# Six more landing buffers for the weights, in the room of queries, keys and values, until the input units' second halves begin

## The chip, the cores and the metric

The kernel runs on one core of a Trainium2 chip. The metric is the device time of one execution in microseconds (us), given as the median of several runs. TensorE (PE) does the matrix products and the transposes, VectorE (DVE), ScalarE (ACT) and GpSimd (POOL) the rest; SyncE (SP) starts nearly all transfers of weights from device memory (HBM).

## The reference, cut to what matters

Two transformer layers over 256 tokens of width 2048, all in float32. Before the first layer, a vector `c` is turned into six vectors of 2048 that shift, scale and gate its two halves:

```python
mod = silu_c @ w_ada[l] + b_ada[l]                 # w_ada: 2048 x 12288, 100 MB
shift_m, scale_m, gate_m, shift_f, scale_f, gate_f = jnp.split(mod, N_MOD, axis=-1)
h = modulate(rmsnorm(x, g_norm_mix[l]), shift_m, scale_m)
proj = h @ w_in[l]                                 # w_in: 2048 x 3904
...                                                # two kinds of attention, heads of 64 and 128
x = x + gate_m[:, None, :] * mix
h = modulate(rmsnorm(x, g_norm_ffn[l]), shift_f, scale_f)
f = jnp.square(jax.nn.relu(h @ w_ff1[l])) @ w_ff2[l]
```

The second layer projects its input by another `w_in`, runs three attention branches (one of them over the 256 rows of `mem`, by `w_mem_kv`) and projects back.

## The kernel before, in words

All work is written as a Python program that puts instructions into one queue for each engine. An engine works its queue in order; a wait for another engine is a semaphore count.

**Weight tiles.** Every large product is cut into units of up to 512 output columns. A unit runs over pairs of 128 input rows: one pair is a tile of 128 x 1024 numbers (512 KB). Its way: SP starts the transfer into a landing buffer (`fetch`), ACT rounds it to a high part `whi` (line 282), DVE subtracts to get the low part `wlo` (line 283), and PE does twelve products with the high and low parts (lines 392, 393 and 397). `consume` issues transfer and split for a tile four tiles ahead of PE; the split of a tile waits until PE has read the tile four before it. When the split is done, the landing buffer is free. The sixteen tiles of `w_mem_kv` go to PE unsplit.

**Ada parts.** The product with `w_ada` (192 parts of 512 KB in 24 columns `c` of 8) is done on DVE: a part is fetched into a landing buffer like a tile, and one instruction multiplies it by `silu(c)` and sums (line 537, `ada_part`). After the eighth part of a column, small instructions (lines 561 to 566, `ada_reduce`) finish its slice of shift or scale.

**Landing buffers.** They are used in turn: `slot % ring`. While `mem` is projected there are nine, five in `raw` and four in `raw_wide`; `narrow()` then sets the ring to five.

**The order of the work.** `run` lays out a unit tile by tile and calls `pump` after each. `pump` first calls `fill`, which puts ada parts into the queues as long as a model in the program says that the part would be done on DVE at most 3 us after PE: the model keeps a clock for each queue (`PE.t`, `DV.t`, `SP.t`), and one for the transfers (`due["dma"]`), which moves on by 0.00303 us a column, 1.55 us for a full tile or a part, and never starts before SP's clock. A transfer whose landing buffer is free only later holds back SP's clock. Where PE's next pair of inputs (`lhs.ready`) waits for a column of ada, `run` puts the parts that are left of it at once (`wanted`, `ada_token`).

**Around the change.** After the two units of `mem`, `modulated(j)` for j = 0 to 7 makes the inputs of `w_in`, two blocks of 128 rows each: it transposes, scales and shifts by the ada columns (line 781, ACT), and splits (lines 787, ACT, and 789, DVE). Pairs 0 to 3 need ada columns 0, 4, 1, 5; pairs 4 and 5 need 2 and 6; pairs 6 and 7 need 3 and 7. So the first halves of the first six units of `w_in` run first (`u_h0`, 24 tiles on pairs 0 to 3), then two whole units (`u_lat`, eight tiles of 512 and eight of 320 columns on pairs 0 to 7), and then the second halves of the six, mixed with the attention heads. The first unit of `u_lat` thus meets pair 6 after 30 tiles. `region2`, 8192 columns, holds `qT`, `kT`, `dv` (columns 0 to 6143), which are first written after a second half, and `lat` (from column 6144), written after `u_lat`; before it was allotted, its room held the inputs of `mem` and `raw_wide`. `fence` is a list of the last instruction of each queue, on which first writers of reused room wait.

Of the kernel before, what the change touches and what calls it, by code (L numbers as in the profile page):

```python
# [8 lines left out]
F32 = mybir.dt.float32  # L9
# [6 lines left out]
P = 128  # L16
D = 2048
EPS = 1e-6
LAM0 = 0.8 - 0.6 * float(np.exp(-0.0))
NRAW, NSPLIT, NWIDE = 5, 4, 4  # L20
MAGIC = 12582912.0
RSEED = float(0x5F3759DF)
TWO_PI = (6.28125, 1.93500518798828125e-3, 3.0199160510240e-7)
# [111 lines left out]
def program(nc, a, out):  # L135
    with ExitStack() as ctx:
        build(nc, ctx, a, out)


def build(nc, ctx, a, out):  # L140
    def sb(name, shape, dt=F32, scope=ctx):
        return scope.enter_context(nc.sbuf_tensor(name, shape, dt))

    def sem(name):
        return ctx.enter_context(nc.semaphore(name))

    due = {}
    PE, AC, DV, PO = (Queue(sem(f"s_{n}"), due, us) for n, us in (("pe", 0.11), ("act", 0.55), ("dve", 0.3), ("pool", 0.8)))
    SP = Queue(None, due, 0.05)
# [50 lines left out]
    def grab(ring):  # L200

        while all(b.busy for b in ring):
            yield
        b = nxt(ring)
        while b.busy:
            b = nxt(ring)
        b.busy = True
        return b
# [46 lines left out]
    slots = [raw[:, i, :] for i in range(NRAW)]  # L255
    raw_sem = [[sem(f"s_raw{i}"), 0] for i in range(NRAW + NWIDE)]
    raw_free = [[] for _ in raw_sem]
    state = dict(slot=0, ring=NRAW + NWIDE, split=0, nsplit=0, unit=0)
    halves, read = {}, {}

    def fetch(src, n):
# [26 lines left out]
    def narrow():  # L288

        state["ring"], state["slot"] = NRAW, 0  # L290
# [7 lines left out]
    def ada_next():  # L298
        c, k0 = adas.popleft()
        i, x, landed = fetch(a["w_ada"][4 * c + k0 // 4, k0 // 2 % 2], 512)  # L300
        raw_free[i] = [ada_part(x, landed, c, k0)]

    def fill():

        while adas:
            i = state["slot"] % state["ring"]
            if raw_free[i] is None:
                break
            issue = max([SP.t] + [due[id(q), v] for q, v in raw_free[i]])
            landed = max(issue, due.get("dma", 0.0)) + 1.55 + 2.0  # L310
            if max(DV.t, landed) + 1.3 > PE.t + 3.0:
                break
            ada_next()
# [4 lines left out]
    def pump(n=1, width=2):  # L318

        for _ in range(n):  # L320
            fill()
            live = 0
            for g in list(bg):
                if live < width or g in started:
                    started.add(g)
                    live += 1
                    if next(g, "end") == "end":
                        bg.remove(g)
# [7 lines left out]
    def mark(name, tok):  # L336

        counts[name] = counts.get(name, 0) + 1
        t_of[name] = tok
# [106 lines left out]
    def turn_rows(bank, blocks, *waits):  # L446

        for i, src in enumerate(blocks):
            o = bank.ap[:, i * P:i * P + P]
            tok = PE.put(lambda e, o=o, s=src: e.transpose(o, s, ident), *waits, bank.free, mark=i == len(blocks) - 1)  # L450
        return tok
# [73 lines left out]
    start = ExitStack()  # L525
# [99 lines left out]
                                             ALU.mult), k)  # L625

    lhs_mem.hi = sb("lhsM", [P, 16, 256], F32, start)
    wide_raw = sb("raw_wide", [P, NWIDE, 1024], F32, start)
    slots += [wide_raw[:, i, :] for i in range(NWIDE)]
    posi = small[:, used[0]:used[0] + 2].bitcast(I32)  # L630
    used[0] += 2
    t_pos = load(AC, posi, a["position_columns"])
# [165 lines left out]
    fence = [PE.tok(), AC.tok(), DV.tok(), PO.tok()]  # L798
    start.close()
    att = ExitStack()  # L800
    region2 = sb("region2", [P, 8192], F32, att)
    part = [region[:, 1024 * i:1024 * i + 1024].rearrange("p (t d) -> p t d", t=2) for i in range(6)]
    omla = region[:, 2048:4096].rearrange("p (t d) -> p t d", t=2)
    odiff = [region[:, 4096 + 1024 * j:5120 + 1024 * j].rearrange("p (t d) -> p t d", t=2) for j in range(2)]
# [12 lines left out]
    def rope(x1, x2, segs, half, c0, tok):  # L817

        cos = trig[:, :, c0:c0 + half].rearrange("p t (a w) -> p t a w", a=1).to_broadcast([P, 2, segs, half])
        sin = trig[:, :, c0 + half:c0 + 2 * half].rearrange("p t (a w) -> p t a w", a=1).to_broadcast([P, 2, segs, half])  # L820
        r = [x[:, 0:2 * segs * half].rearrange("p (t s w) -> p t s w", t=2, w=half) for x in rot]
        w = [tok, t_of["trig"], [DV.tok()]]
        ks = [DV.put(lambda e, o=o, i0=i0, i1=i1: e.tensor_tensor(o, i0, i1, ALU.mult), *w, us=0.2)
              for o, i0, i1 in ((r[0], x1, cos), (r[1], x2, sin), (r[2], x2, cos), (r[3], x1, sin))]
        DV.put(lambda e: e.tensor_tensor(x1, r[0], r[1], ALU.subtract), ks, us=0.2)
        return DV.put(lambda e: e.tensor_tensor(x2, r[2], r[3], ALU.add), ks, us=0.2)

    def normed(r, ks, n, d0, extra=()):

        ssq, rq = sm(2), sm(2)  # L830
        j = yield from grab(tmps)
        for t in range(2):
            k = AC.put(lambda e, t=t: e.activation(j.ap[:, 0:n], r.ap[:, t, 0:n], ACT.Square,
                                                   accum_out=ssq[:, t:t + 1]), ks, j.free, [AC.tok()])
        j.release([k])
        yield
        k = rsqrt(ssq, 2, 1.0 / n, rq, k)
        for t in range(2):
            k = DV.put(lambda e, t=t: e.tensor_scalar(lat[:, t, d0:d0 + n], r.ap[:, t, 0:n], rq[:, t:t + 1], None,
                                                      ALU.mult), k, fence)  # L840
        t_of["lat", d0] = k
        mark("lat", k)
# [5 lines left out]
    def g_kvlat(r, ks):  # L848
        kr = rope(r.ap[:, :, 256:288].rearrange("p t (s w) -> p t s w", s=1),
                  r.ap[:, :, 288:320].rearrange("p t (s w) -> p t s w", s=1), 1, 32, 16, ks)  # L850
        kr = DV.put(lambda e: e.tensor_copy(r.ap[:, :, 320:384], r.ap[:, :, 256:320]), kr)
        yield from normed(r, ks, 256, 512)
        yield
        b = yield from grab(SB)
        tok = turn_rows(b, [r.ap[:, t, 256:384] for t in range(2)], kr)
        yield
        mark("krT", AC.put(lambda e: e.activation(krT, b.ap[:, 0:256], ACT.Copy), tok, hn_sq.free))
        b.release([t_of["krT"]])
        r.release([tok, t_of["lat", 512]])
# [177 lines left out]
    def row_unit(u, **kw):  # L1037
        par, tok = run(u, **kw)
        r = take(rows)
        return r, evac2(par, tok, u["n"], r.ap[:, :, 0:u["n"]], r.free)  # L1040
# [70 lines left out]
    bg.append(g_lat(r, ks))  # L1111
    r, ks = row_unit(u_lat[1], width=3)
    bg.append(g_kvlat(r, ks))
    halved = set()
    for kind, i in order1:
        if kind == "h":
# [8 lines left out]
        else:  # L1125
            if i == 0:
# [3 lines left out]
                fence = [PE.tok(), AC.tok(), DV.tok(), PO.tok()]  # L1130
# [30 lines left out]
    fence = [PE.tok(), AC.tok(), DV.tok(), PO.tok()]  # L1161
# [129 lines left out]
    fence = [PE.tok(), AC.tok(), DV.tok(), PO.tok(), t_of["xf"]]  # L1291
# [287 lines left out]
    fence = [PE.tok(), AC.tok(), DV.tok(), PO.tok()]  # L1579
# [148 lines left out]
```

How the kernel before makes its waits and increments, by code:

```python
    def run(self, eng):  # L106
        seen = {}
        for waits, fn, sem, by in self.items:
            for s, v in waits:
                if v > seen.get(id(s), 0):
                    eng.wait_ge(s, v)
                    seen[id(s)] = v
            ins = fn(eng)
            if sem is not None:
                ins.then_inc(sem, by)
# [1535 lines left out]
    @block.sync  # L1651
    def _(eng):
        SP.run(eng)
        eng.wait_ge(*t_out)
```

## Time and profile before

| | |
|---|---|
| median of 3 runs | 2173.46 us (2172.63 to 2175.14) |
| the profiled execution's own time | 2174.42 us |
| its span in the trace | 2172.6 us |
| PE busy | 1992.0 us (92%) |
| DVE busy | 1314.6 us (61%) |
| ACT busy | 944.5 us (43%) |
| mean granted clock of PE | 0.967 |
| moved by transfers | 448.82 MB, mean 207 GB/s |

Busy times are those of one profiled execution. Instructions are named by engine, line of the kernel and operation, with what they write and read. In square brackets stands how long the engine was idle before the instruction, and what released it. The granted clock is 1.00 at full speed (2.4 GHz) and 0.50 at half (1.2 GHz).

### The profile page before, as it was taken

Reading aid. Unit: us, or ns where it says so; the run is one execution under the profiler, and the core shown is the slowest. Engines: PE = TensorE matmul, PEld = TensorE weight load, DVE = VectorE, ACT = ScalarE, POOL = GpSimd, SP = SyncE. Lnnn points to the kernel's source line nnn. Section 1 sums busy time; section 2 is a strip of 40 time slices with the busy share of each in tenths; the row PEclk is TensorE's granted clock in tenths of the full one; section 3 lists DMA queues with packets and bytes.
Section 4 is the critical chain, followed back from the end, with each engine's and each line's share of the span. In section 5 each row is a group of like instructions: output and inputs, shape, how many; then the busy total and the mean of one; then the engine's idle time right before and its main releaser. Section 6 shows DMA issues by size and latency. Waiting matters only on the chain. (4 is left out here: it accounts for less than half of the span.)

```text
span 2172.6 us, 24527 instructions
## 1 busy us (share of the span) xinstructions
PE 1992.0 (92%) x9240; PEld 1635.6 (75%) x9240; DVE 1314.6 (61%) x2057; ACT 944.5 (43%) x1440; POOL 156.6 (7%) x118
## 2 busy tenths in 40 slices
PE   6697896868799999999999999989989999999999
PEld 3376775646577888888888878879888787787877
DVE  3877776776796555555555555567555555545544
ACT  2553444333444344434434445445434444444433
POOL 0000000001100110110010022110100001101000
PEclk9898999879899999999999999999999999999999
DMA  9998675757897555555555565534534456656644
GB/s 354 340 319 294 230 262 194 242 189 262 299 340 261 190 193 185 192 194 184 187 194 190 185 197 172 160 113 139 160 106 150 135 170 190 192 182 187 194 172 168
DMA packets 128967, 448.82 MB, mean 207 GB/s; under 512 B 14288, under 2 KB 14544, under 8 KB 128336
## 3 DMA queue, kind: packets, MB, share of 16 engines
q1 hardware_dynamic: 124928, 433.74, 60.1%
q0 software_dynamic: 1568, 7.34, 0.9%
q10 hardware_dynamic: 2352, 6.17, 0.7%
q8 instruction: 72, 1.18, 0.2%
q14 instruction: 47, 0.39, 0.1%
HBM read 443.00 MB, written 4.19 MB: 206 GB/s over the span
## 5 line engine op out<-in xcount | busy, mean ns | idle before, releaser
L283 DVE TENSOR_TENSOR wlo<-raw,whi 128x1024 fp32r<-128x1024 f32 (+4 forms) x652 | 787.1, 1211 | 736.8 <-ACT whi L282 691.0
L282 ACT ACTIVATE whi<-raw 128x1024 fp32r<-128x1024 f32 (+4 forms) x652 | 657.8, 1011 | 849.4 <-PE g L397 710.5
L392 PE MATMUL g<-whi,lhsA_hi 128*128 128x512 f32 (+4 forms) x1840 | 714.3, 390 | 41.5 <-DVE lhsA_lo L789 34.1
L393 PE MATMUL g<-whi,lhsA_lo 128*128 128x512 f32 (+4 forms) x1840 | 695.5, 380 | 0.0
L397 PE MATMUL g<-wlo,lhsA_hi 128*128 128x512 f32 (+4 forms) x1840 | 467.2, 376 | 0.0
L392 PEld LDWEIGHTS g<-whi,lhsA_hi 128*128 128x128 f32 x1840 | 355.4, 193 | 105.2 <-ACT tmp L781 27.6
L393 PEld LDWEIGHTS g<-whi,lhsA_lo 128*128 128x128 f32 x1840 | 355.5, 193 | 53.7 <-issue 1.4
L397 PEld LDWEIGHTS g<-wlo,lhsA_hi 128*128 128x128 f32 x1840 | 341.6, 191 | 55.9 <-DVE wlo L283 0.2
L537 DVE SCALAR_TENSOR_TENSOR raw<-raw,srow 128x1024 f32<-128x1024 f32 x181 | 216.6, 1219 | 20.5 <-DMA raw<-in_w_ada 20.1
L392 PE MATMUL g<-whi,lhsF_hi 128*128 128x512 f32 x512 | 200.6, 392 | 0.0
L393 PE MATMUL g<-whi,lhsF_lo 128*128 128x512 f32 x512 | 199.3, 389 | 0.0
L397 PE MATMUL g<-wlo,lhsF_hi 128*128 128x512 f32 x512 | 136.9, 389 | 0.0
L1177 POOL TENSOR_TENSOR region<-region,tmp 128x512 f32<-128x512 f32 x40 | 62.5, 1582 | 728.6 <-DVE tmp L1173 718.4
L397 PEld LDWEIGHTS g<-wlo,lhsF_hi 128*128 128x128 f32 x512 | 96.1, 188 | 20.1
L392 PEld LDWEIGHTS g<-whi,lhsF_hi 128*128 128x128 f32 x512 | 96.2, 188 | 19.6
L393 PEld LDWEIGHTS g<-whi,lhsF_lo 128*128 128x128 f32 x512 | 96.1, 188 | 19.6
L392 PE MATMUL g<-whi,lhsY_hi 128*128 128x512 f32 x128 | 50.6, 395 | 0.0
L393 PE MATMUL g<-whi,lhsY_lo 128*128 128x512 f32 x128 | 50.3, 393 | 0.0
L392 PE MATMUL g<-whi,yz_hi 128*128 128x512 f32 x128 | 49.8, 389 | 0.0
L393 PE MATMUL g<-whi,yz_lo 128*128 128x512 f32 x128 | 49.8, 389 | 0.0
L1626 POOL TENSOR_TENSOR y<-y,tmp 128x512 f32<-128x512 f32 x16 | 27.1, 1713 | 264.4 <-DVE tmp L1620 264.4
L724 POOL TENSOR_TENSOR hn_sq<-row 128x384 f32<-128x384 f32 (+2 forms) x18 | 19.5, 1103 | 302.8 <-ACT row L458 232.6
(250 smaller groups left out, 1473.2 us busy)
## 6 DMA issues: line engine op xcount, KB each, us to landing
raw<-in_w_ff SPq DMA_DIRECT2D x256, 512.0 KB, 3.5
raw<-in_w_ada SPq DMA_DIRECT2D x181, 512.0 KB, 5.0
raw<-in_w_in SPq DMA_DIRECT2D x176, 512.0 KB, 4.2
raw<-in_w_out SPq DMA_DIRECT2D x64, 512.0 KB, 5.0
raw<-in_w_in SPq DMA_DIRECT2D x80, 384.0 KB, 3.1
raw<-in_w_branch_a SPq DMA_DIRECT2D x12, 512.0 KB, 3.7
raw<-in_w_branch_b SPq DMA_DIRECT2D x12, 512.0 KB, 4.3
raw_wide<-in_w_ada SPq DMA_DIRECT2D x11, 512.0 KB, 8.3
```

The source lines that it names most:

```text
L282: t_hi = AC.put(lambda e: e.activation(hi, x, ACT.Copy), landed, free, us=0.2 + n * 0.00167)
L283: t_lo = DV.put(lambda e: e.tensor_tensor(lo, x, hi.bitcast(F32), ALU.subtract), landed, t_hi, free, us=0.15 + n * 0.00208)
L392: PE.put(lambda e, o=o, x=xh, w=h, f=first: e.matmul(o, x, w, start=f, stop=False), w, mark=False, us=us)
L393: PE.put(lambda e, o=o, x=xl, w=h: e.matmul(o, x, w, start=False, stop=False), mark=False, us=us)
L397: tok = PE.put(lambda e, o=o, x=xh, w=l, f=end and kk == 1: e.matmul(o, x, w, start=False, stop=f), t_lo, mark=kk == t == 1, us=us)
L537: b.tok = DV.put(lambda e: e.scalar_tensor_tensor(out=src, in0=src, scalar=0.5, in1=sv, op0=ALU.mult, op1=ALU.mult, accum_out=b.ap[:, i:i ...
L724: k = PO.put(lambda e, t=t: e.tensor_tensor(sq[:, segs * t:segs * t + segs], v[:, t], v[:, t], ALU.mult), tok, sq_.free)
L1177: k = PO.put(lambda e, xc=xc, tm=tm: e.tensor_tensor(xc, xc, tm.ap[:, :], ALU.add), k, x_tok[j])
L1626: k = PO.put(lambda e, yt=yt, tm=tm: e.tensor_tensor(yt, yt, tm.ap[:, :], ALU.add), k, y.tok[t])
```

## The change

Six columns of 1024 of `region2`, the room of `qT`, `kT` and `dv`, become landing buffers 5 to 10 as soon as `region2` is allotted; the ring is eleven until both units of `u_lat` are laid out, and then five again. The first use of each new buffer waits for `fence`. After the ring is five again a new `fence` is taken, on which the first writers of `qT`, `kT` and `dv` wait. During the units of `mem` the ring is nine as before. In `fill` the model takes 0 for a token that it has no time for.

```diff
-NRAW, NSPLIT, NWIDE = 5, 4, 4
+NRAW, NSPLIT, NWIDE = 5, 4, 6
...
-    state = dict(slot=0, ring=NRAW + NWIDE, split=0, nsplit=0, unit=0)
+    state = dict(slot=0, ring=NRAW + 4, split=0, nsplit=0, unit=0)
...
-            issue = max([SP.t] + [due[id(q), v] for q, v in raw_free[i]])
+            issue = max([SP.t] + [due.get((id(q), v), 0.0) for q, v in raw_free[i]])
...
-    wide_raw = sb("raw_wide", [P, NWIDE, 1024], F32, start)
-    slots += [wide_raw[:, i, :] for i in range(NWIDE)]
+    wide_raw = sb("raw_wide", [P, 4, 1024], F32, start)
+    slots += [wide_raw[:, i, :] for i in range(4)]
...
     region2 = sb("region2", [P, 8192], F32, att)
+    slots[NRAW:] = [region2[:, 1024 * i:1024 * i + 1024] for i in range(6)]
+    raw_free[NRAW:NRAW + 6] = [fence] * 6
+    state["ring"] = NRAW + 6
...
     bg.append(g_kvlat(r, ks))
+    narrow()
+    fence = [PE.tok(), AC.tok(), DV.tok(), PO.tok()]
     halved = set()
```

## Rows read from the trace of the kernel before

**Rows 1.** The page's first part: busy time, share of span, instructions of each engine.
```profile
PE 1992.0 (92%) x9240; PEld 1635.6 (75%) x9240; DVE 1314.6 (61%) x2057; ACT 944.5 (43%) x1440; POOL 156.6 (7%) x118
```

**Rows 2.** Stretches: length; PE, PEld, DVE, ACT, POOL busy; clock, DMA share, GB/s.
```profile
60.00:70.00 10.00, 9.73 (x23) 3.70 (x21) 7.73 (x28) 6.69 (x17) 0.00 (x0) 1.00 1.02 390
...
130.00:140.00 10.00, 10.00 (x46) 8.29 (x45) 7.92 (x11) 5.33 (x6) 0.00 (x0) 1.00 1.00 350
...
150.00:160.00 10.00, 10.00 (x45) 8.29 (x45) 7.17 (x10) 5.71 (x8) 0.00 (x0) 1.00 0.79 282
...
190.00:200.00 10.00, 0.00 (x0) 0.00 (x0) 7.92 (x16) 1.05 (x3) 0.00 (x0) 0.69 0.96 367
```

**Rows 3.** PE's instructions in order of time: start, length, instruction, idle before.
```profile
99.43 0.77 PE L392 MATMUL g<-whi,lhsA_hi 128*128 128x512 f32 x1 [14.21 <-DVE lhsA_lo L789]
...
202.03 0.77 PE L392 MATMUL g<-whi,lhsA_hi 128*128 128x512 f32 x1 [13.01 <-DVE lhsA_lo L789]
...
250.69 0.66 PE L450 MATMUL pS<-cst,region 128*128 128x128 f32 x4 [2.72 <-DVE lhsA_lo L441]
```

**Rows 4.** Waits from 99 to 202 us: total us, times, longest.
```profile
PE g L392 <- DVE lhsA_lo L789: 28.8, 3, 14.2
...
SPq L98 <- DVE wlo L283: 48.5, 30, 4.2
...
ACT whi L282 <- DMA raw<-in_w_in: 27.7, 18, 3.0
```

**Rows 5.** All engines in order of time, around the wait before 202 us.
```profile
184.32 1.22 DVE L537 SCALAR_TENSOR_TENSOR raw<-raw,srow 128x1024 f32<-128x1024 f32 x1
184.35 1.07 PE L397 MATMUL g<-wlo,lhsA_hi 128*128 128x512 f32 x4
185.05 1.69 ACT L282 ACTIVATE whi<-raw 128x1024 fp32r<-128x1024 f32 x2 [1.38 <-DMA raw<-in_w_in]
...
187.07 1.07 PE L397 MATMUL g<-wlo,lhsA_hi 128*128 128x512 f32 x4
...
189.79 0.74 ACT L282 ACTIVATE whi<-raw 128x640 fp32r<-128x640 f32 x1 [3.05 <-DMA raw<-in_w_in]
...
190.61 0.82 DVE L283 TENSOR_TENSOR wlo<-raw,whi 128x640 fp32r<-128x640 f32 x1 [0.16 <-issue]
191.58 1.22 DVE L537 SCALAR_TENSOR_TENSOR raw<-raw,srow 128x1024 f32<-128x1024 f32 x1
...
193.69 1.23 DVE L537 SCALAR_TENSOR_TENSOR raw<-raw,srow 128x1024 f32<-128x1024 f32 x1 [0.87 <-DMA raw<-in_w_ada]
...
198.69 0.08 DVE L537 DVE_READ_ACCUMULATOR raw<-raw,srow 128x1 f32 x1
```

**Rows 6.** DVE in order of time, ada parts one behind the other.
```profile
82.98 1.22 DVE L537 SCALAR_TENSOR_TENSOR raw_wide<-raw_wide,srow 128x1024 f32<-128x1024 f32 x1
...
84.13 1.22 DVE L537 SCALAR_TENSOR_TENSOR raw_wide<-raw_wide,srow 128x1024 f32<-128x1024 f32 x1
```

**Rows 7.** Line 537 alone: length, DVE busy (instructions, two a part), clock, DMA, GB/s.
```profile
89.40:189.00 99.60, 31.24 (x51) 0.92 0.89 313
...
202.00:250.00 48.00, 12.01 (x20) 0.94 0.76 250
```

**Rows 8.** PE by the microsecond around 202 us: length, busy, clock, DMA share, GB/s.
```profile
202.00:203.00 1.00, 0.97 (x2) 0.50 0.46 184
...
207.00:208.00 1.00, 1.00 (x5) 0.76 0.87 119
```

**Rows 9.** Transfers by kind: KB each, median us from issue to landing.
```profile
raw<-in_w_ada SPq DMA_DIRECT2D x181, 512.0 KB, 5.0
...
raw_wide<-in_w_ada SPq DMA_DIRECT2D x11, 512.0 KB, 8.3
```

**Rows 10.** DVE and SP in order of time, before the first part of column 2.
```profile
89.22 0.16 DVE L566 SCALAR_TENSOR_TENSOR mods<-mods,vec 128x4 f32<-128x4 f32 x1
89.67 5.07 SPq L98 DMA_DIRECT2D raw<-in_w_ada  x3
```

## The prediction

> **What bounds the kernel now.** I read the busy times first: PE works 92% of the span [rows 1], so time can only come out of its idle 8% or its clock. Next the stretches of 10 us between 90 and 250 us, where the new buffers are in use: the reader is to see that from 112 us on PE is busy in each of them without a break (10.00 of 10.00, also where the transfers fall to 282 GB/s), until it stands still from 189 to 202 us [rows 2]. Third, PE's own order of time: one wait of 14.21 us before the first product of the input units, one of 13.01 us before pair 6 of the first latent unit, and then none over 0.4 us until 250.69 [rows 3]; the grouped waits say that all 28.8 us of waiting there (these two and a third of 1.6 us) end with line 789, the low part of the modulated inputs [rows 4]. Last SP and ACT: SP waits 48.5 us on splits before it can start the next transfer, and ACT 27.7 us on tiles that haven't landed [rows 4]. So five buffers do hold the transfers back, but on PE's path that shows only where an ada column is late.
>
> The first long wait is outside the change's reach: the transfers for its tiles go into buffers 0 to 3, as before, and it ends by the modulated inputs of columns that were fetched in the ring of nine. The second is the one that counts: pairs 6 and 7 need ada column 7.
>
> **What hangs on the 13 us.** PE ends its last tile at 187.07 + 1.07 = 188.14, and some transposes at 189.02. DVE then still has the split of the tile four ahead (190.61 to 191.43) and five parts of column 7: the first starts at 191.58, the last ends with its sum at 198.69 + 0.08 = 198.77 [rows 5]. From there 202.03 - 198.77 = 3.26 us go to the column's small instructions, the modulation and its split; this tail doesn't change.
>
> **Edit 1, the ring of eleven: what it gives on the chip with the order unchanged.** Three things in that stretch come from late landings.
> - ACT starts the high parts of the tiles at 185.05 after waiting 1.38 us for a transfer, which holds DVE. With data there, DVE's queue runs: a part 184.32 to 185.46 (1.22 with its follower overlapped, see below), the split of the first tile 1.14 to 186.6; the next, of 320 columns, needs PE's read at 184.35 + 1.07 = 185.42, has its high part by 186.2 and is done at 187.35; two parts to 189.65. ACT's last high part waited 3.05 us for its transfer until 189.79 [rows 5]; without that it waits for PE's 188.14 and is done by 188.9. DVE's last split then runs 189.65 to 190.4 instead of to 191.43: 1.0 us gained.
> - The five parts took 198.77 - 191.43 = 7.34 us, as each waited for its transfer (0.87 us at one, the others 0.1 each) [rows 5]. Parts that have landed follow each other at 84.13 - 82.98 = 1.15 us [rows 6]; five are 5.75 us. Gained: 1.6 us.
> - Have they landed? They must come out of slack before 189. Transfers ran at 313 GB/s between 89 and 189 us [rows 7], and at 390 in the ring of nine [rows 2]; at that rate the same bytes take 100 x 313/390 = 80 us. With eleven buffers SP starts a part eleven fetches behind instead of five, six times 99.6 us over some 60 fetches = 1.66 us, some 10 us earlier. So yes.
>
> Together 2.6 us.
>
> **Edit 1, on the order.** `fill` knows the number of buffers through SP's clock in the model. Up to pair 6 of the latent unit 27 parts were laid out beside 30 tiles, three of them against the five that were left (25 to 26 by 189 us, from 51 instructions [rows 7]). The model's transfer clock alone allows (2.72 - 1.55)/1.55 = 0.75 part a tile, 2.72 us being PE's twelve products at the code's own price; 30 x 0.75 = 23, and three more at the start where PE is seen late. So the transfer clock (1.55 us a transfer, whatever the chip does) sets the admission nearly everywhere, not the buffers. Only where DVE's clock jumps (the norm of the memory keys, then the split of tile 38) does a buffer come free late in the model: following its arithmetic there, SP's clock is held once by 2.7 us, and by under 1 us at three other tiles, 4 us in all. Without that, the DVE condition (done at most 3 us after PE) takes over, and I get one part more before pair 6, four left instead of five; two at most, none at least, since the sum comes within 0.1 us of the limit at three tiles. A part more before the wait is worth 1.15 us [rows 6], as DVE has room in front: 7.17 us busy of 10 at 150, 7.92 at 130 [rows 2].
>
> Sum: 2.6 + 1.15 = 3.75 us, with 2.6 and 4.9 as ends from the admission. The wait shrinks from 13.0 to 9.3 us. It stays long enough for the clock to fall as now: the wait of 13 us left PE at half clock from 202 to within the 207th microsecond [rows 8], and I take the same 5.8 us behind the new one, so 0 with 1 us either way for where the clock's steps fall.
>
> The rest of the way to 250.69 is PE without a wait [rows 3], so what is gained at 202 arrives there, and from there on order and durations are those of before but for the places of ada parts.
>
> **The rule against it.** The ada transfers take 5.0 us from issue to landing in the ring of five, 8.3 in `raw_wide` [rows 9]. The Trainium skill ("DMA: Bandwidth & Descriptors", section "Anatomy of one DMA") puts a transfer at about 2 us fixed plus its bytes at 436 GB/s, an estimate of 3.2 us for 512 KB. By that rule a buffer would be busy some 6 us with its split, and five of them would outrun the port: buffers would hold nothing back, and the ring would change nothing (the first rival). The trace has 5.0, and ACT waiting 27.7 us; it speaks for the buffers.
>
> **Edit 2, the first wait on `fence`.** Buffer 5 is first fetched for the second part of column 2. SP starts column 2 at 89.67 now, and the last instruction of DVE in the fence, the end of column 5, is over at 89.22 + 0.16 = 89.38 [rows 10]. Cost 0; behind it in SP's queue would be every later tile, and at worst, if something older than I see is in the fence, 1 us, beside a PE that waits until 99.43 for other things.
>
> **Edit 3, back to five and the new fence.** By then 82 to 84 fetches were made, so the last used buffer is number 4, 5 or 6 of eleven: buffer 0 was used five to seven fetches before, as in a ring of five. Cost 0; if it were the buffer just used, the tile's transfer would start after a split that waits for PE four tiles back, take 5.0 us [rows 9] and 2.3 for the split, some 10 us against the 10.9 that four tiles give: still 0. The new fence is passed long before the first write of `qT` (four tiles, 10.9 us later): 0. `narrow` issues nothing.
>
> **How it stands to the runs.** From the profiled execution 2174.42 - 3.75 = 2170.7; it is 0.96 us above the median, so the median forecast is 2173.46 - 3.75 = 2169.7.
>
> **Rivals.**
> - *The buffers don't matter on the path* (0.24): the last parts are bound by the memory's rate (370 GB/s or so in that stretch, 367 in rows 2) and not by when they start, since DVE, with its own load of 80%, consumes them no sooner, and `fill` lays out the same order. For it: the five parts came every 1.29 us, the transfers' pace. Against: 27.7 us of landings waited for. Then 0 to -1.5: 2173.
> - *The order gives more* (0.16): in the model the freed clock takes three or four parts more before pair 6, so that one or two are left. For it: parts have a place on DVE. Against: the 0.75 a tile. Then 2.6 + 4 x 1.15 = 7.2: 2166.3.
> - *The shifted parts cost more later* (0.14), slower than before: after 202 us `fill` starts from other clocks, and a part comes to stand in front of a low part that PE waits for, as at 250.69, where PE waits 2.72 us on line 441 [rows 3]. One such part costs 1.15 us; where it makes a wait long enough for half clock, up to 2.9 us more, half of the 5.8 us [rows 8], 4.05 together. Three net of those removed: 12.2 - 3.75 = +8.4, 2181.9. It decides from three on; two leave +4.35. For it: DVE holds both kinds in one queue, 12 us of parts lie between 202 and 250 alone [rows 7]. Against: the share of parts a tile stays.
>
> **The numbers.** What a measurement here tells from no change is 0.2%, 4.35 us: below 2169.1 is faster, above 2177.8 slower. The forecast (0.46) has a range of its own of 2167.5 to 2172. It lies just short of the bound: of its 0.46 some 0.19 are faster, the rest same. Faster: 0.19 + 0.16 = 0.35 and 0.02 of the first rival's scatter, 0.37. Slower 0.14. Same 0.49. The range 2165 to 2174.5 leaves out the slower rival and little below.
>
> **What would show it.** Right: PE still waits once before pair 6 of the latent unit, near 189 us, 8 to 10.5 us long; the parts right before its end follow each other at 1.15 us with no wait for a transfer, three to five of them; ACT's waits for landings between 99 and 202 us fall from 27.7 to under 8 us, and SP's waits shrink; the first product still comes at 99.4; half clock for 5 to 6 us behind the wait; PE's waits between 250 and 620 us sum to the same within 4 us. Wrong: parts still 1.3 us apart (the first rival); a wait under 7 us (the second); more waits on lines 441, 789, 450 after 230 us (the third); a new wait of SP at the first use of buffer 5, or at tile 60.

## The result and the profile after

The changed kernel takes 2168.09 us, the median of 12 runs (2164.51 to 2173.80), beside 2174.68 us for the kernel before on the same chip (12 runs, 2172.63 to 2180.76). The ratio is 0.9968 [0.9957, 0.9978]: 0.32% faster, some 6.6 us. In another set of runs on another chip it was 0.9972 [0.9961, 0.9983]. The forecast of 2169.7 us was 1.6 us too high; the gain was bigger than forecast (6.6 against 3.75 us). That the time was missed by less than the gain is in part luck: the forecast started from a median of 2173.46 us for the kernel before, and in this comparison that kernel took 1.2 us more.

The profiled execution took 2169.46 us, 4.96 less than that of before, with a span of 2167.7 us (before 2172.6) and a mean granted clock of 0.965 (before 0.967). The page's busy times, beside [rows 1]:

```profile
PE 1998.6 (92%) x9240; PEld 1642.9 (76%) x9240; DVE 1311.8 (61%) x2057; ACT 944.2 (44%) x1440; POOL 156.7 (7%) x118
```

No engine has more instructions or fewer. PE is busy 6.6 us longer for the same 9240, so it ran them at a lower clock somewhere; its idle time fell by 11.5 us (180.6 to 169.1). What that was is seen below. PE's own order of time, beside [rows 3]:

```profile
98.97 0.77 PE L392 MATMUL g<-whi,lhsA_hi 128*128 128x512 f32 x1 [14.00 <-DVE lhsA_lo L789]
...
195.34 0.76 PE L392 MATMUL g<-whi,lhsA_hi 128*128 128x512 f32 x1 [7.57 <-DVE lhsA_lo L789]
...
242.08 0.66 PE L450 MATMUL pS<-cst,region 128*128 128x128 f32 x4 [1.84 <-DVE lhsA_lo L441]
```

The three places are the same and so are their releasers. The first wait stands (14.21 to 14.00), the second went from 13.01 to 7.57 us, and 250.69 has become 242.08. The grouped waits from 99 to 202 us, beside [rows 4] (total us, times, longest; PE's row of [rows 4] takes in the wait that ends at 202.03):

```profile
PE g L392 <- DVE lhsA_lo L789: 23.1, 3, 14.0
...
ACT whi L282 <- PE g L397: 36.6, 24, 3.9
...
SPq L98 <- DVE wlo L283: 45.6, 31, 4.2
SPq L98 <- DVE raw L537: 19.2, 15, 5.5
```

ACT's 27.7 us of waiting for landed tiles are gone: no row of ACT names a transfer any more, what it waits for is PE. SP still waits on splits and parts, and hardly less in sum (48.5 to 45.6 us on splits). That is no contradiction: with all buffers full SP must wait for one, only that now it is eleven fetches ahead. The stretch before the wait's end, all engines, beside [rows 5]:

```profile
187.00 0.74 ACT L282 ACTIVATE whi<-region 128x640 fp32r<-128x640 f32 x1 [1.98 <-PE g L397]
...
187.83 0.82 DVE L283 TENSOR_TENSOR wlo<-region,whi 128x640 fp32r<-128x640 f32 x1 [0.75 <-issue]
188.57 1.22 DVE L537 SCALAR_TENSOR_TENSOR region<-region,srow 128x1024 f32<-128x1024 f32 x1
...
189.71 1.22 DVE L537 SCALAR_TENSOR_TENSOR region<-region,srow 128x1024 f32<-128x1024 f32 x1
...
190.86 1.22 DVE L537 SCALAR_TENSOR_TENSOR region<-region,srow 128x1024 f32<-128x1024 f32 x1
...
192.00 0.08 DVE L537 DVE_READ_ACCUMULATOR region<-region,srow 128x1 f32 x1
```

ACT's last high part is released by PE and not by a transfer. Behind DVE's last split stand three parts of column 7 where five stood, 1.14 and 1.15 us apart and none with a wait. From their end, 192.08, to PE's 195.34 are 3.26 us, the same tail as before. In windows, line 537 alone (length, DVE busy with its instructions, clock, DMA share, GB/s), beside [rows 7]:

```profile
89.40:189.00 99.60, 35.48 (x59) 0.93 0.95 359
...
202.00:250.00 48.00, 10.44 (x18) 0.93 0.61 217
```

313 GB/s became 359, and 51 instructions of parts 59. And PE by the microsecond behind the wait (length, PE, PEld, DVE, ACT, POOL busy, clock, DMA share, GB/s), beside [rows 8]:

```profile
196.00:197.00 1.00, 1.00 (x4) 0.81 (x3) 0.92 (x2) 0.05 (x1) 0.00 (x0) 0.50 0.00 0
...
198.00:199.00 1.00, 1.00 (x5) 0.77 (x4) 1.00 (x3) 0.00 (x0) 0.00 (x0) 0.72 0.08 20
199.00:200.00 1.00, 1.00 (x6) 0.84 (x5) 1.00 (x3) 0.08 (x1) 0.00 (x0) 1.00 0.86 246
```

The 199th microsecond has clock 0.72, so full speed (2.4 GHz) is back at about 198.56, 3.2 us behind PE's start; before it was back at about 207.48 (0.76 in the 208th), 5.45 us behind. The 0.00 of the DMA share says that no transfer runs: all eleven buffers are in use, and SP starts the next one at 197.94 us, as soon as the first part behind the modulation (196.69 to 197.91) has freed its buffer. Before, with five buffers, the transfers stood still at the same place, from 203 to 205 us; so this is no sign of the new ring.

**Where the time went, by landmarks.** The same PE instructions bound the stretches in both traces (for the round numbers at 1320 and 1620 us to within 0.2 us). Length, PE busy with its instructions, clock, DMA share, GB/s; before:

```profile
99.43:250.69 151.26, 133.98 (x619) 0.94 0.85 295
250.69:525.90 275.21, 212.82 (x949) 0.89 0.66 226
525.90:586.93 61.03, 49.28 (x205) 0.89 0.77 284
586.93:1320.00 733.07, 722.11 (x3240) 0.99 0.62 206
1320.00:1620.00 300.00, 273.95 (x1592) 0.97 0.47 143
1620.00:2172.60 552.60, 535.28 (x2469) 0.99 0.54 172
```

and after:

```profile
98.97:242.08 143.11, 132.14 (x618) 0.96 0.84 312
242.08:520.60 278.52, 215.87 (x949) 0.88 0.65 226
520.60:579.91 59.31, 49.16 (x205) 0.90 0.79 284
579.91:1312.60 732.69, 723.20 (x3240) 0.99 0.62 206
1312.60:1614.80 302.20, 278.08 (x1592) 0.96 0.46 142
1614.80:2167.70 552.90, 535.43 (x2469) 0.99 0.53 172
```

The first stretch holds the change and is 8.15 us shorter: 5.44 of the wait, 1.1 from the earlier full speed ((5.45 - 3.2)/2, since at half clock half the time is lost), 0.9 at the wait on line 441 (2.72 to 1.84), the rest in small pieces. The second stretch is 3.3 us longer than before, the third 1.7 shorter, the fifth 2.2 longer. In the second and the fifth PE has the same number of instructions and is busy 3.05 and 4.13 us longer: what is lost there is clock and no new wait. How much of that belongs to the change is asked below, with a second trace of the same kernel.

### The profile page after: what moved, and what is told of

It is laid out like the page before. It is cut to its first block and busy times, and to the rows that moved or that the text cites. A ratio compares the mean times of both kernels' runs of the same rounds, so it can differ in the third digit from the quotient of the medians.

```text
span 2167.7 us, 24528 instructions
## 1 busy us (share of the span) xinstructions
PE 1998.6 (92%) x9240; PEld 1642.9 (76%) x9240; DVE 1311.8 (61%) x2057; ACT 944.2 (44%) x1440; POOL 156.7 (7%) x118
## 5 line engine op out<-in xcount | busy, mean ns | idle before, releaser
L283 DVE TENSOR_TENSOR wlo<-raw,whi 128x1024 fp32r<-128x1024 f32 (+3 forms) x631 | 761.5, 1211 | 727.8 <-ACT whi L282 687.0
L282 ACT ACTIVATE whi<-raw 128x1024 fp32r<-128x1024 f32 (+3 forms) x631 | 637.9, 1013 | 818.2 <-PE g L397 719.5
L537 DVE SCALAR_TENSOR_TENSOR raw<-raw,srow 128x1024 f32<-128x1024 f32 x160 | 190.8, 1219 | 16.3 <-DMA raw<-in_w_ada 16.1
```

The lines of the kernel that those rows point to most:

```text
L282: t_hi = AC.put(lambda e: e.activation(hi, x, ACT.Copy), landed, free, us=0.2 + n * 0.00167)
L283: t_lo = DV.put(lambda e: e.tensor_tensor(lo, x, hi.bitcast(F32), ALU.subtract), landed, t_hi, free, us=0.15 + n * 0.00208)
L537: b.tok = DV.put(lambda e: e.scalar_tensor_tensor(out=src, in0=src, scalar=0.5, in1=sv, op0=ALU.mult, op1=ALU.mult, accum_out=b.ap[:, i:i ...
```

## The experiments

The theory: more buffers let the landings run ahead, so that splits and parts at 180 to 199 us don't wait; and the model, with a freer SP clock, lays out more parts before pair 6. The rivals were the three of the prediction. In the kernels that separate the two, the planner has a ring of its own (`vslot`, `vring`, its own list of free times), beside the chip's.

**The order alone.** Five buffers on the chip, the order of the changed kernel:

```diff
-    state = dict(slot=0, ring=NRAW + 4, split=0, nsplit=0, unit=0)
+    state = dict(slot=0, ring=NRAW + 4, split=0, nsplit=0, unit=0, vslot=0, vring=NRAW + 4)
+    vfree = [[] for _ in raw_sem]
...
-            issue = max([SP.t] + [due.get((id(q), v), 0.0) for q, v in raw_free[i]])
+            issue = max([SP.t] + [due.get((id(q), v), 0.0) for q, v in vfree[j]])
...
-    state["ring"] = NRAW + 6
+    vfree[NRAW:NRAW + 6] = [fence] * 6
+    state["vring"] = NRAW + 6
```

> The order of the instructions is that of the changed kernel (the planner reckons with eleven buffers), but on the chip only five buffers are used until the second halves. My theory (the gain at the wait before pair 6 is two parts: earlier landings 2.6 us, two parts fewer behind the last split 2.3 us): the wait of PE is 13.0 - 2 x 1.29 = 10.4 us, since the three parts left still come at the pace of their transfers, and the kernel is 2 to 3.5 us faster than before. Rival 'order alone': the wait is 7.6 us as in the changed kernel and the gain is the whole 6.6 us. Rival 'buffers alone': the wait is 13 us and the gain 0.

Measured: 2180.11 us, 1.0017 [1.0008, 1.0026], where 2 to 3.5 us less than before were expected; the wait before pair 6 was 11.72 us and not 10.4, and ACT still waited 28.7 us for landings. But it has a fault of its own: when `narrow()` sets the turn back to buffer 0 after a run in a ring of five, the next fetch takes a buffer that was just used. PE shows it in a wait that neither kernel has:

```profile
231.91 0.44 PE L456 MATMUL pS<-cst,row 128*128 128x128 f32 x2 [2.08 <-DVE row L861]
```

So the run was made again without setting back the chip's turn.

```diff
-        state["ring"], state["slot"] = NRAW, 0
+        if state["ring"] != NRAW:
+            state["ring"], state["slot"] = NRAW, 0
```

> As e1_order_only (order of the changed kernel, five buffers on the chip), but the turn of the chip's buffers is not set back to buffer 0 when the second halves begin. In e1_order_only that setting back made SP wait from 218.3 to 223.0 us for a buffer that had just been filled, and PE 2.1 us at 231.9. My theory: the wait before pair 6 stays near 11.7 us (the three parts left come at the pace of their transfers, and the last tile lands late), the wait at 232 us goes, and the kernel takes the time of before within 2 us, as the order alone costs some 1 to 2 us of clock and waiting after 300 us. Rival: the order needs the buffers, with or without the jump: PE still waits at 232 us or loses over 2 us between 205 and 325 us.

Measured: 2177.14 us, 1.0005 [0.9994, 1.0016], and a wait of 13.04 us where 11.7 were expected. PE in the first kernel and in this one:

```profile
200.12 0.77 PE L398 MATMUL g<-whi,lhsA_hi 128*128 128x512 f32 x1 [11.72 <-DVE lhsA_lo L795]
```

```profile
200.24 0.76 PE L399 MATMUL g<-whi,lhsA_hi 128*128 128x512 f32 x1 [13.04 <-DVE lhsA_lo L796]
```

The two kernels differ only in the turn that is set back when the second halves begin, so up to this wait their instructions are the same: 11.72 and 13.04 are two executions of one order. Column 7's last sum ended at 196.86 and 196.98 us in them, but PE had stopped at 188.40 and 187.20. DVE in order of time in the second:

```profile
188.61 0.82 DVE L288 TENSOR_TENSOR wlo<-raw,whi 128x640 fp32r<-128x640 f32 x1
189.86 1.23 DVE L544 SCALAR_TENSOR_TENSOR raw<-raw,srow 128x1024 f32<-128x1024 f32 x1 [0.42 <-DMA raw<-in_w_ada]
...
192.66 1.22 DVE L544 SCALAR_TENSOR_TENSOR raw<-raw,srow 128x1024 f32<-128x1024 f32 x1 [0.41 <-DMA raw<-in_w_ada]
...
194.50 1.23 DVE L544 SCALAR_TENSOR_TENSOR raw<-raw,srow 128x1024 f32<-128x1024 f32 x1 [0.61 <-DMA raw<-in_w_ada]
195.75 1.23 DVE L544 SCALAR_TENSOR_TENSOR raw<-raw,srow 128x1024 f32<-128x1024 f32 x1
```

Three parts are left behind the last split instead of five, but of the last four parts three wait for their transfers. Up to the last part of column 7 the same number of transfers must be made, in whatever order, and with five buffers they are what is late; a part moved forward mostly moves the waiting. At this wait the order by itself is worth 0 to 1.3 us (13.01 before, 13.04 and 11.72 here), and neither kernel is faster than the one before.

**The buffers alone.** Eleven on the chip, while the planner goes on with five. In the first kernel the planner's turn was set back at `narrow()` too, so that its order agrees with that of before only up to the last tile of `u_lat`; in the second it is that of before to the end.

```diff
     state["ring"] = NRAW + 6
```

This line is that of the changed kernel; what is new is that `vring` stays `NRAW`. The second kernel has this in `narrow()` besides:

```diff
-        state["vring"], state["vslot"] = NRAW, 0
+        if state["vring"] != NRAW:
+            state["vring"], state["vslot"] = NRAW, 0
```

> Eleven buffers on the chip, but the planner reckons with five, so the order of the instructions is that of the kernel before. My theory: five parts are left behind the last split, at 1.15 us each with nothing to wait for, the wait of PE is 13.0 - 2.6 = 10.4 us, and the kernel is 2 to 3.5 us faster than before. Rival 'order alone': the wait stays 13 us, gain 0. Rival 'buffers alone': the wait is 7.6 us, gain 6.6 us.

> As e2_buffers_only, but the planner's turn is not set back either when the second halves begin, so the order is that of the kernel before to the very end (in e2_buffers_only it left it there). My theory: the wait before pair 6 is 10.2 us as in e2_buffers_only, half clock behind it 3.4 us shorter, and the kernel is 4 to 6 us faster than before. Rival: the gain of e2_buffers_only came from its order after 220 us; then this one is 3 us faster or less.

Measured: 2170.51 us, 0.9973 [0.9963, 0.9982], and 2171.33 us, 0.9984 [0.9974, 0.9995]. In both the wait was 10.17 us, near the 10.4 and 10.2 expected, and ACT waited for no transfer. The gains, 4.8 and 3.3 us, missed their forecasts (2 to 3.5, and 4 to 6) on either side. PE in the second:

```profile
199.85 0.76 PE L399 MATMUL g<-whi,lhsA_hi 128*128 128x512 f32 x1 [10.17 <-DVE lhsA_lo L796]
```

The landings alone are worth 13.01 - 10.17 = 2.84 us of the wait; the forecast's term was 2.6. DVE's order of time there shows the burst of five, from its first part to its last sum:

```profile
190.78 1.22 DVE L544 SCALAR_TENSOR_TENSOR region<-region,srow 128x1024 f32<-128x1024 f32 x1
...
196.50 0.09 DVE L544 DVE_READ_ACCUMULATOR region<-region,srow 128x1 f32 x1
```

So each wait is three pieces: from PE's stop to the burst, the burst, the tail. Before: 2.56 (189.02 to 191.58) + 7.19 + 3.26 = 13.01. With the buffers: PE stopped at 189.68, so 1.10 + 5.81 + 3.26 = 10.17. Changed, with PE's stop at 187.77: 0.80 + 3.51 + 3.26 = 7.57. The landings alone are worth 2.84 us of the wait (1.46 at the burst's start, 1.38 in its pace), and with them the new order takes off another 2.60 (two parts, 2.30, and 0.30 at the start). Alone the two halves bring 2.84 and 0 to 1.3 us of the wait, together 5.44.

The wait's length also depends on when PE stopped. From the first product of the input units to pair 6 it took 102.60 us before, 101.13 and 102.21 with the order alone, 98.61, 99.69 and (seven buffers, below) 99.91 with buffers alone, and 96.37 and 96.69 with both (the changed kernel's two traces). By this measure the order alone is worth 0.4 to 1.5 us, the buffers alone 2.7 to 4.0, the two added 3.1 to 5.5, and both in one kernel 5.9 to 6.2 (5.5 with eight buffers, below). The kernel before has one trace only, so these sizes are rough.

**How many buffers.** A ring of eight for chip and planner (its edit is shown), and later one of seven (`NRAW + 2`) on the chip alone with the order of before.

```diff
-    state["ring"] = NRAW + 6
+    state["ring"] = NRAW + 3
```

> Three more buffers instead of six, planner and chip alike; by the planner three parts are left before pair 6, as with eleven. My theory: three more buffers already bring the transfers ahead by three fetches of some 1.7 us, 5 us, more than the landings were late (1.4 and 3.1 us), so the wait is 7.5 to 8 us and the time that of the changed kernel within 1.5 us. Rival 'all six are needed': ACT still waits over 10 us for landings between 99 and 190 us, the wait is 9 us or more, and half of the gain is lost.

> Seven buffers on the chip instead of eleven, order of the kernel before to the end as in e2b_buffers_same_order. The landings were late by 1.4 and 3.1 us with five buffers; two more bring a transfer forward by two fetches of 1.66 us, 3.3 us. My theory: ACT's waits for landings nearly go and the wait before pair 6 is 10.2 to 10.8 us, so two more do what six do. Rival: the transfers need a deeper queue to come at 1.3 us each; then the wait is over 11.3 us and ACT still waits over 8 us for landings between 99 and 202 us.

Measured: with eight 2169.12 us, 0.9969 [0.9958, 0.9979], wait 7.57 us, and one wait of ACT of 0.8 us for a landing; with seven 2170.20 us, 0.9977 [0.9967, 0.9987], wait 10.16 us, none of ACT. Eight do what eleven do, and two more than five give all that six more give at this wait, as both expectations had it. The transfer rate went on rising with the number, 331 GB/s from 89.4 to 189 us with seven, 349 with eleven in the same order, while the time didn't: what lands beyond DVE's need is only stored.

**The planner's price of a transfer.** It reckons 1.55 us where the trace after has 1.46 (512 KB at 359 GB/s). A price of 1.38 lets it put in more parts. Applied to the changed kernel, and to the kernel before:

```diff
-        return i, x, SP.dma(x, src, raw_sem[i], free, us=n * 0.00303)
+        return i, x, SP.dma(x, src, raw_sem[i], free, us=n * 0.0027)
...
-            landed = max(issue, due.get("dma", 0.0)) + 1.55 + 2.0
+            landed = max(issue, due.get("dma", 0.0)) + 1.38 + 2.0
```

> The changed kernel, with a transfer of 512 KB priced at 1.38 us instead of 1.55 in the planner. By the planner column 7 is then complete before pair 6 and no part is left behind the last split. My theory (the planner's transfer price sets how many parts go in front, and each part left costs 1.15 us): the wait before pair 6 falls from 7.6 us by three parts, 3.4 us, to some 4.2 us, PE may keep full speed, and the time is 3.5 to 7 us under the changed kernel. Rival 'DVE is full': the parts then lie in front of the splits and PE waits for low parts between 112 and 187 us by as much as is saved; the time is that of the changed kernel or above.

> The kernel before with five buffers, but a transfer priced at 1.38 us in the planner, so that it lays out all of column 7 before pair 6, as e4_cheaper_transfers did with eleven buffers (wait 3.15 us there). My theory: five buffers bring a transfer every 1.66 us and no faster; 5 transfers more before 189 us come some 8 us late, so the wait before pair 6 (or waits for tiles before it) sums to 8 to 10 us, and the kernel is 1 to 4 us faster than before, 5 us slower than e4_cheaper_transfers. Rival: the price alone does it, and buffers are not needed: wait 3 to 4 us, gain 8 us or more.

Measured: with the new buffers 2166.94 us, 0.9956 [0.9944, 0.9969], no part of column 7 left at the wait, which is 3.15 us. PE didn't keep full speed: 3.4 us of half clock followed, and by the ratios the gain over the changed kernel is 2.6 us, not the 3.5 to 7 expected; the two intervals overlap. With five buffers 2179.05 us, 1.0020 [1.0008, 1.0031]: slower, where 1 to 4 us of gain were expected, although its wait before pair 6 fell to 9.37 us. ACT there waits longer for landings than before (27.7 us in [rows 4]):

```profile
ACT whi L282 <- DMA raw<-in_w_in: 41.0, 24, 3.4
```

The planner took transfers for cheaper than five buffers made them (322 GB/s in that stretch), and the tiles came later to ACT. Up to pair 6 this cost PE nothing that its trace shows: it has no wait over 0.2 us between 112.33 and the one of 9.37 us, and from the first product to pair 6 it took 99.53 us, 3.1 less than before. So the loss lies further on, and its cause isn't shown: the profiled execution, at 2174.78 us, was the fastest of its twelve runs.

**The cheap price up to the second halves only**, so that the later stages keep the planner's old price:

```diff
-    state = dict(slot=0, ring=NRAW + 4, split=0, nsplit=0, unit=0)
+    state = dict(slot=0, ring=NRAW + 4, split=0, nsplit=0, unit=0, price=0.0027)
...
-        return i, x, SP.dma(x, src, raw_sem[i], free, us=n * 0.00303)
+        return i, x, SP.dma(x, src, raw_sem[i], free, us=n * state["price"])
...
-            landed = max(issue, due.get("dma", 0.0)) + 1.55 + 2.0
+            landed = max(issue, due.get("dma", 0.0)) + 512 * state["price"] + 2.0
...
     narrow()
+    state["price"] = 0.00303
```

> The changed kernel with a transfer priced at 1.38 us only until the second halves begin, and 1.55 us after. My theory: the wait before pair 6 is 3.15 us with 3.4 us of half clock behind it as in e4_cheaper_transfers, 11 us ahead of before by 205 us, and nothing of what e4_cheaper_transfers lost again between 550 and 670 us, so 3 to 6 us faster than the changed kernel. Rival: what is gained there is lost again in the later stages whatever the price; then the time is that of e4_cheaper_transfers.

> The kernel of e6_cheap_until_halves again, beside the changed kernel. My theory: 3 to 4.5 us faster than the changed kernel in this comparison too (wait of 3.1 instead of 7.6 us, at most 1.7 us of half clock less behind it, part of it lost after 550 us). Rival: both are the same within 1.5 us, and the difference of the two ratios so far (0.9949 and 0.9968) was chance.

> The changed kernel itself once more, beside e6 on the same chip. Expected: 0.9968 of before within its interval, wait before pair 6 of 7.6 us.

Measured: 2164.60 us, 0.9949 [0.9932, 0.9966]; again, on another chip, 2163.29 us, 0.9949 [0.9935, 0.9963]. There the changed kernel ran beside it: 2169.24 us, 0.9972 [0.9961, 0.9983], with its wait of 7.56 us. PE and line 537 in the repeated run:

```profile
190.62 0.48 PE L392 MATMUL g<-whi,lhsA_hi 128*128 128x512 f32 x1 [3.14 <-DVE lhsA_lo L789]
```

```profile
89.40:189.00 99.60, 38.65 (x64) 0.94 0.97 376
```

3.14 us is a little less than the tail of 3.26 us behind the last part: column 7 is complete when PE arrives, and what is left is the column's small work and the modulation. This version beats both kernels, by 10.5 us the kernel before (2173.77 us in that set) and by 6 us the changed one beside it. Its intervals in the two sets end at 0.9966 and 0.9963, those of the changed kernel begin at 0.9957 and 0.9961, so they overlap by a little; that 0.9949 came twice speaks for a difference. The gain over the changed kernel, 6 us here, is above the 3 to 4.5 us forecast. Whether the price has to go back at the second halves isn't shown: 0.9956 [0.9944, 0.9969] with the cheap price throughout isn't told apart from 0.9949.

## Why the prediction was right, and where its sizes were off

- **The place and the mechanism.** PE still waits once, before pair 6, for column 7, and the gain comes from there. The working of the landings holds: ACT's last high part now waits for PE, the parts follow each other at 1.15 us instead of 1.3. Term forecast 2.6 us (1.0 from the splits, 1.6 from the pace), measured 2.84 (1.46 and 1.38) with the order held still.
- **The admission was mis-sized.** The term was one part, 1.15 us, with two as its upper end; three parts were left in place of five, so it was two, and the wait fell by 2.60 us for it. So the wait of 7.57 us lies outside the 8 to 10.5 us that the prediction gave as its sign of being right, though above the 7 us of the rival. The count that I followed through the model's clocks stood within 0.1 us of the limit at three tiles, which the prediction says; a term decided by so little should have been taken half way to its upper end. The rival of three or four parts did not come about.
- **The clock behind the wait** was set to 0 with 1 us either way: it gave 1.1 us in the first trace and 0.9 in the second. Of the 5.8 us of half clock that the prediction read, [rows 8] show 5.45 (0.76 in the 208th microsecond puts the step at 207.48), and it expected 5 to 6 us again. Behind 7.57 us it was 3.2 us, behind 7.56 in the second trace 3.6. That the shorter wait is the cause isn't shown: with the old buffers and a wait of 11.72 us it was 3.2 too (the list is in the last section). With the right admission this is the other piece of what the forecast of the local sum lacked: 3.75 against 2.84 + 2.60 + 1.1 = 6.5 us, of which up to 1.1 may be scatter. That 6.5 is near the 6.6 of the medians is chance, as the first stretch gave 8.15 and later ones lost part of it again.
- **From there to the end** the forecast had order and durations as before. To 250.69 that held and better (line 441 waits 0.9 us less). The two longest waits from there to 620 us stand:

```profile
520.60 0.80 PE L392 MATMUL g<-whi,lhsA_hi 128*128 128x512 f32 x1 [7.35 <-ACT whi L282]
...
579.91 1.09 PE L450 MATMUL pS<-cst,row 128*128 128x128 f32 x4 [10.15 <-DVE row L1208]
```

  Before they were 7.39 and 11.75 us. PE's idle time in the second and third stretch together went from 74.14 to 72.80 us, within the 4 us forecast. But the two stretches took 1.6 us longer (336.24 to 337.83), through PE's busy time. The changed kernel's second trace takes them apart again:

```profile
244.11:520.97 276.86, 219.89 (x948) 0.86 0.66 227
520.97:580.28 59.31, 48.42 (x204) 0.90 0.78 284
```

  There they took 336.17 us, as before (in the ten other traces 335.8 to 339.1), though the clock was lower still (0.86) and PE busy 4 us longer than in the first trace: what the lower clock added to busy time came out of waits that were there anyhow. So that 1.6 us is the scatter of one execution, and the order isn't shown to cost anything here. The fifth stretch is the same. Summed by the same products of unit tiles (from the 4300th to the 5700th, a sum over the traces), it took 319.7 us before and 322.0 and 322.2 in the two traces of the changed kernel. But with the order of before to the end it took 320.6 (eleven buffers) and 322.8 (seven), and in two traces of the kernel with the cheap price up to the second halves 322.4 and 320.4. The scatter of one kernel is as large as the difference, and the longest of the thirteen has the order of before: no cost of the changed order is shown here either.
- **Edit 2, the first wait on the fence:** 0, as forecast; the first product came at 98.97 us and SP has no new wait there. **Edit 3, back to five:** 0 in the changed kernel, which by the prediction's count comes after 82 to 84 fetches. But the turn that is set back is a hazard, as the order-alone kernel showed (1.0017 with it, 1.0005 without; the intervals overlap): I priced that case at 0, and it showed as a new PE wait of 2.08 us.
- **The rivals.** That the buffers don't matter fell: with before's order they bring 0.9984 and 0.9973, seven of them 0.9977. By the rule of the Trainium skill ("DMA: Bandwidth & Descriptors", "Anatomy of one DMA"), worked out ahead of the run to an estimate of 3.2 us for a transfer, five would have been enough. That section gives its fit for transfers that GpSimd issues, and these are issued by SP. The trace of before had 5.0, and here the measurement decides. Slower from shifted parts did not come about: after 230 us the longest waits of PE that line 441 ends are 2.8 us in both traces, and the one on line 789 went from 4.4 to 4.2 us.

How the total of 6.6 us divides is known only roughly, since a run of a kernel scatters by several us: the buffers with the order of before to the end bring 0.16% and 0.23% of the 0.32% (eleven and seven of them), 3.5 to 5 us, and 0.27% where the order is that of before only up to the second halves; the order on top of them the rest, with intervals that overlap; the order alone nothing.

## What to carry to other kernels

Landing buffers and the planner's order belong together: the buffers alone took 2.84 us off the wait, the order alone 0 to 1.3 and nothing off the time, and both together 5.44. Two more buffers did the buffers' share, and then the planner's price of a transfer was the next limit (with a lower one 0.9956, and 0.9949 where it holds only up to the second halves; with five buffers the lower price gave 1.0020). Where a wait of PE is made shorter, look at the clock behind it and in the stages after it, as PE's busy time for the same instructions tells it, and take a second trace of the same kernel before a difference of 1 to 3 us there is put down to the change.

## What the runs showed of the hardware that I had not expected

- One core's transfers held 359 GB/s over 99.6 us with eleven landing buffers, and 376 with more of them asked for; five buffers held 313 to 322, seven 331, eight 347. The time from issue to landing rose with the rate: for the ada transfers between 90 and 190 us the median was 5.3 us before, 5.6 to 5.8 in the changed kernel (old and new buffers alike), and 7.0 (old) and 8.3 (new) at 376 GB/s. The waits of ACT for landings were gone all the same. The new buffers' medians with their first transfers, which start at 89.15 us, taken in:

```profile
region<-in_w_ada SPq DMA_DIRECT2D x21, 512.0 KB, 6.0
region<-in_w_in SPq DMA_DIRECT2D x15, 512.0 KB, 6.3
```

- How long half clock lasts behind the wait before pair 6 doesn't follow from the wait's length. In the thirteen traces it was 5.0 and 5.45 us behind waits of 13.0, 3.2 behind 11.72, 3.6, 4.9 and 5.1 behind 10.2, 5.4 behind 9.37, 3.2, 3.6 and 4.1 behind 7.6, and 3.4 behind each of the three of 3.1 (worked out from the granted clock by the microsecond, as above). For the shortest, in the repeated kernel with the cheap price, PE by the microsecond (length, busy, clock, DMA share, GB/s) shows the clock fall only when PE is at work again:

```profile
189.00:190.00 1.00, 0.00 (x0) 1.00 0.96 380
190.00:191.00 1.00, 0.38 (x2) 0.97 1.03 389
191.00:192.00 1.00, 1.00 (x4) 0.50 0.51 200
...
194.00:195.00 1.00, 1.00 (x5) 0.83 0.66 154
```

  PE starts at 190.62 at full clock and has half of it from about 190.94 to 194.34, 3.4 us. So a wait of 3.14 us still cost 1.7 us of clock, behind its end.
- The same kernel's two traces have PE busy 215.87 us (949 instructions recorded) and 219.89 us (948) between the same two of its waits, in stretches of 278.52 and 276.86 us: there the clock and the waits hide each other, and neither busy time nor clock alone tells what a stretch lost.
